# Opening pair of experts in the order gate, gate, up, up, down, with two up units in places used once

## The chip, the cores and the metric

One program runs on one core of a Trainium2 chip. The core has a matrix engine (TensorE, PE in the profile), a vector engine (VectorE, DVE), a scalar engine (ScalarE, ACT), GpSimd (POOL) and SyncE (SP), whose queue issues nearly all transfers from HBM to SBUF. Sixteen DMA engines carry these transfers. The metric is the device time of the program in microseconds (us), the median of several runs.

## The reference, cut to what matters

Two layers over 256 tokens of width 1024, in float32: a recurrent block with a dense feed-forward block, then attention with an expert block. Only the expert block is touched here: 8 experts, each token goes to its best two, and each expert is a SwiGLU of width 3584.

```python
def swiglu(h, w_gate, w_up, w_down):
    return (jax.nn.silu(h @ w_gate) * (h @ w_up)) @ w_down
...
    logits = (t @ router).astype(jnp.float32)
    top_v, top_i = lax.top_k(logits, TOP_K)
    w = jax.nn.softmax(top_v, axis=-1)
...
    for e in range(N_EXPERTS):
        out = out + combine[:, e:e + 1].astype(t.dtype) * swiglu(t, w_gate[e], w_up[e], w_down[e])
```

The weights of the 8 experts are 24 matrices of 1024 x 3584 float32, 14.7 MB each, 352 MB in all.

## The kernel before

**Units.** Each expert matrix is cut in eight units of 1792 KB, one DMA each, so an expert block has 192 loads. A gate or up unit is 128 rows of the matrix, and all eight are summed in PSUM. A down unit is three and a half "rows" of a [128 x 28 x 1024] view; the half row is finished with the next unit, so an even down unit is given back a little late.

**Pairs.** Experts are sorted by the number of their tokens and handled in four pairs: one large (96 token slots, 3 groups of 32) and one small (64 slots, 2 groups). Below, GL, UL and DL are the gate, up and down units of the large expert (0 to 7 each), GS and US those of the small one. Down units of the small expert are computed in the next pair (DE, "EARLIER" in the code). A pair in the middle takes its 48 units in the order GL, DE 0 to 3, UL, DE 4 to 7, GS, DL 0 to 3, US, DL 4 to 7. The opening pair has no DE, hence 40 units: GL, UL, GS, DL 0 to 3, US, DL 4 to 7. Its large expert is always expert 1 (`FIRST`), so it can be loaded before routing is known; the small one can't.

**Places.** A unit lies in one of 8 places of a ring (`PERMANENT`), 7 of them in the tensor `ring` and one `ring_last`. A load into a place waits until TensorE has used the unit that lay there (semaphore `used`, which counts finished units), so a new load is issued at each finished unit, in order. The first eleven units of the opening are loaded while attention still runs, each as soon as its memory is free: eight in the ring, three in places that are used once, `ring_a`, `ring_b` and `ring_c` (`BESIDE_A` to `BESIDE_C`). When a unit in such a place is finished, no load follows. `OPENED` says where the eleven lie: GL 0 and 1, GL 2 in `ring_b`, GL 3, GL 4 in `ring_a`, GL 5 to 7, UL 0 and 1, UL 2 in `ring_c`.

**Order.** Each engine runs its own list, written by hand. SP issues loads in the order in which TensorE takes the units (`pair_loads` for all but the eleven). On TensorE, `summed` computes a gate or up unit, `lowered` a down unit; `pair` is the order of a pair. PSUM banks 0 to 5 hold the three sums of the large expert, banks 0 to 3 the two of the small one, so the next matrix waits until ScalarE (`silus`) or VectorE (`products`) has read each bank pair (`acc_free`). `selection_transposes` prepares the scatter to tokens; `gather` fetches the tokens of the next pair in the midst of DL 4 and 5.

Of the kernel before, what the change touches and what calls it, by code (L numbers as in the profile page):

```python
# [24 lines left out]
KT = D // P  # L25
# [4 lines left out]
UK = 4  # L30
# [3 lines left out]
E = 8  # L34
# [62 lines left out]
def downs(job, steps):  # L97

    return [("D", job, n) for n in steps]


def pair_units(opening):

    def sums(kind, job):
        return [(kind, job, n) for n in range(KT)]
    early, late = (range(EARLY), range(EARLY, PARTS))
    return (sums("G", LARGE) + ([] if opening else downs(EARLIER, early)) + sums("U", LARGE)
            + ([] if opening else downs(EARLIER, late)) + sums("G", SMALL) + downs(LARGE, early)
            + sums("U", SMALL) + downs(LARGE, range(EARLY, PARTS)))


OPENING_UNITS, UNITS = pair_units(True), pair_units(False)
LAST_UNITS = downs(EARLIER, range(PARTS))
PAIR_UNITS = len(UNITS)
assert PAIR_UNITS % RING == 0 and len(OPENED) == RING + 3


class Group:
# [16 lines left out]
    def col(self, later=0):  # L135
        return at(2 * (self.ahead + later), 2, self.i)

    def later(self, i):
        return self.before + i - len(OPENED)

    def slot(self, i):
        n = self.later(i)
        return OPENED[n] if n < 0 else PERMANENT[n % RING]

    def landed(self, i):
        n = self.later(i)
        return 16 if n < 0 else at(16 * (n // RING + 2), 16 * PAIR_UNITS // RING, self.i)

    def free(self, i):
        n = self.later(i)  # L150
# [18 lines left out]
def hybrid_trunk(nc, x, norm_mix, norm_ffn, lru_w_in, lru_conv_w, lru_conv_b, lru_w_a, lru_b_a, lru_w_x, lru_b_x,  # L169
                 lru_log_lambda, lru_w_out, fox_w_in, fox_b_f, fox_q_gain, fox_k_gain, fox_w_out, ffn_w_gate,  # L170
                 ffn_w_up, ffn_w_down, moe_router, moe_w_gate, moe_w_up, moe_w_down, out):
    with ExitStack() as ctx:
# [138 lines left out]
        def of_group(a):  # L311
# [37 lines left out]
        arrived = [sem(f"arrived{i}") for i in range(len(OPENED))]  # L349
# [47 lines left out]
        def _(sp):  # L397
# [24 lines left out]
            def pair_loads(group):  # L422
                experts = {LARGE: slice(FIRST, FIRST + 1)} if group is OPENING else {}
                for i, (kind, job, n) in enumerate(group.table):
                    if group is OPENING and i < len(OPENED):
                        continue
                    if job not in experts:
                        if group is OPENING:
                            sp.wait_ge(listed, 1)
                        col = group.col(-1) + 1 if job == EARLIER else group.col() + job  # L430
                        experts[job] = bass.ds(sp.value_load(ids[0:1, bass.ds(col, 1)], min_val=0, max_val=E - 1), 1)
                    sp.wait_ge(used, group.free(i))
                    load(group, i, experts[job])
# [6 lines left out]
                    else:  # L440
                        sp.wait_ge(used, n + 1)

            def open_unit(i):
                load(OPENING, i, slice(FIRST, FIRST + 1))

            dense_done(2, 3, 4, 5)
            open_unit(0)
            open_unit(1)
            sp.wait_ge(scored, 8)
            open_unit(2)  # L450
            dense_done(0, 1, 2)
            open_unit(3)
            sp.wait_ge(o_T, 4)
            open_unit(4)
            dense_done(11, 12)
            open_unit(5)
            dense_done(6, 7)
            open_unit(6)
            dense_done(7, 8, 9)
            open_unit(7)  # L460
            dense_done(9, 10, 11)
            open_unit(8)
# [68 lines left out]
        def _(act):  # L531
# [252 lines left out]
            def silus(group, job):  # L784
                for a in range(GROUPS[job]):
                    if a < GROUPS[job] - 1:
                        act.wait_ge(m_part, group.nth((1, 5)[job] + a, 6))
# [14 lines left out]

            def pair(group, following):
                silus(group, LARGE)
                if group is not OPENING:
                    y_copy(SMALL, group.through("D", EARLIER, PARTS - 1))
                selection_copy(group, LARGE)
                silus(group, SMALL)
# [21 lines left out]
        def _(pe):  # L830
# [406 lines left out]

            def acc_free(group, kind, job, a):

                if kind == "U":  # L1240
                    pe.wait_ge(m_silu, group.nth((1, 4)[job] + a, ALL))
                elif job == SMALL:
                    pe.wait_ge(m_act, group.nth(1 + a, ALL))
                elif group is not OPENING and a < GROUPS[SMALL]:
                    pe.wait_ge(m_act, group.nth(a - 1, ALL))

            def summed(group, kind, job, n):
# [72 lines left out]
            def pair(group, following):  # L1320
                for n in range(KT):
                    if group is OPENING:
                        if n % UK == 0:
                            pe.wait_ge(m_x, 1 + n // UK)
                    elif n == 0:
                        pe.wait_ge(m_x, group.nth(2, 2))
                    summed(group, "G", LARGE, n)
                if group is not OPENING:
                    lowered_earlier(group, range(EARLY))
                for n in range(KT):  # L1330
                    summed(group, "U", LARGE, n)
                if group is not OPENING:
                    lowered_earlier(group, range(EARLY, PARTS))
                for n in range(KT):
                    summed(group, "G", SMALL, n)
                    if n == 1 and group is not OPENING:
                        scatter(group)
                    if n == 4:
                        pe.wait_ge(m_Sw, group.nth(1))
                        if group is OPENING:  # L1340
                            pe.wait_ge(m_act, group.nth(3, ALL))
                        else:
                            pe.wait_ge(m_acc, group.nth(0))
                        selection_transposes(group, LARGE)
                pe.wait_ge(m_aT, group.nth(GROUPS[LARGE], ALL))
                for n in range(EARLY):
# [4 lines left out]
                for n in range(KT):  # L1351
                    summed(group, "U", SMALL, n)
                for n in range(EARLY, PARTS):
                    lowered(group, LARGE, n)
                    if following is not None and n < EARLY + 2:
                        if n == EARLY:
                            pe.wait_ge(m_ST, group.nth(2, 2))
                            pe.wait_ge(m_S, following.nth(1))
                        else:
                            pe.wait_ge(m_x, following.nth(1, 2))  # L1360
                        gather(following, n - EARLY)

            pe.wait_ge(m_S, 1)
            pe.wait_ge(hn_hi_done, 2)
            gather_part(0, 4, hn_hi, True, False)
# [4 lines left out]
            pair(OPENING, SECOND)  # L1370
# [26 lines left out]
        def _(dve):  # L1397
# [498 lines left out]
            def products(group, job):  # L1896
                for a in range(GROUPS[job]):
                    if a < GROUPS[job] - 1:
                        dve.wait_ge(m_part, group.nth((3, 6)[job] + a, 6))
# [9 lines left out]
            def pair(group, following):  # L1909
# [3 lines left out]
                products(group, LARGE)  # L1913
                if group is not OPENING:
                    accumulate(group)
                if following is not None:
                    one_hot(group, following)
                products(group, SMALL)

            pair(OPENING, SECOND)  # L1920
            pair(SECOND, Group(0, 2))
# [44 lines left out]
```

## Time and profile before

| | us |
|---|---|
| median of 3 runs | 1338.05 (1337.34 to 1338.09) |
| the profiled execution's own time | 1338.2 |
| its span | 1336.4 |
| PE busy | 1271.3 (95%) |
| DVE busy | 363.3 (27%) |
| ACT busy | 284.5 (21%) |
| POOL busy | 30.9 (2%) |
| HBM read over the span | 325 GB/s in the mean |

The profile cuts the span into 40 slices of 33.4 us; the rows on DMA and on GB/s say for each how busy the 16 DMA engines were, in tenths, and what they moved. A matrix multiplication in float32 stands in the trace as two records, so a unit of GL or UL (24 instructions) is 48 records and one of GS or US (16 instructions) is 32. The queue of SP shows when a load was issued; another view says how long it took from there to its landing.

### The profile page before, as it was taken

Reading aid. Unit: us, or ns where it says so; the run is one execution under the profiler, and the core shown is the slowest. Engines: PE = TensorE matmul, PEld = TensorE weight load, DVE = VectorE, ACT = ScalarE, POOL = GpSimd, SP = SyncE. Lnnn points to the kernel's source line nnn. Section 1 sums busy time; section 2 is a strip of 40 time slices with the busy share of each in tenths; the row PEclk is TensorE's granted clock in tenths of the full one; section 3 lists DMA queues with packets and bytes.
Section 4 is the critical chain, followed back from the end, with each engine's and each line's share of the span. In section 5 each row is a group of like instructions: output and inputs, shape, how many; then the busy total and the mean of one; then the engine's idle time right before and its main releaser. Section 6 shows DMA issues by size and latency. Waiting matters only on the chain.

```text
span 1336.4 us, 27795 instructions
## 1 busy us (share of the span) xinstructions
PE 1271.3 (95%) x12897; PEld 766.0 (57%) x12897; DVE 363.3 (27%) x470; ACT 284.5 (21%) x357; POOL 30.9 (2%) x34
## 2 busy tenths in 40 slices
PE   7999999999999999999999999899998799989897
PEld 7978888888888884335534434344344254344344
DVE  6976444445654363020100200100110100020010
ACT  5855444443545530000000000000000000000000
POOL 2000000000230000000000000000000000000000
PEclk9999999999999999999999999999999999999999
DMA  9556555554441298899999999999999999999994
GB/s 338 171 167 227 185 184 184 188 188 157 157 127 64 87 424 339 319 401 425 426 425 425 425 425 425 427 424 426 426 424 426 426 425 426 425 425 425 425 425 198
DMA packets 70323, 435.53 MB, mean 326 GB/s; under 512 B 4656, under 2 KB 6816, under 8 KB 45632
## 3 DMA queue, kind: packets, MB, share of 16 engines
q1 hardware_dynamic: 69744, 433.10, 81.0%
q8 instruction: 101, 1.65, 0.5%
q0 software_dynamic: 368, 0.63, 0.2%
q14 instruction: 14, 0.11, 0.0%
q10 hardware_dynamic: 96, 0.03, 0.0%
HBM read 432.69 MB, written 1.05 MB: 325 GB/s over the span
## 4 chain that ended last, share of the span: by engine, by line
PE 73%; DMA 23%; ACT 2%; DVE 1%; issue 1%; SPq 0%; POOL 0%; DVEq 0%; ACTq 0%
PE ps L1258 25%; DMA ring<-in_moe_w_down_dram 16%; PE ps L1275 13%; PE ps L839 9%; PE ps L841 9%; PE ps L840 9%; DMA ring<-in_moe_w_gate_dram 6%; PE ps L1229 1%; PE ps L1069 1%; PE ps L1096 1%; PE ps L855 1%; PE ps L881 1%; PE ps L871 1%; PE ps L868 1%; PE ps L870 1%
## 5 line engine op out<-in xcount | busy, mean ns | idle before, releaser
L1258 PE MATMUL ps<-ring,xg 128*32 128x512 f32 (+1 forms) x4384 | 423.1, 540 | 26.6 <-DMA ring<-in_moe_w_up_dram 16.1
L1258 PEld LDWEIGHTS ps<-ring,xg 128*32 128x32 f32 x4384 | 140.1, 110 | 299.6 <-issue 251.3
L1423 DVE TENSOR_TENSOR wlo<-raw,whi 128x2048 fp32r<-128x2048 f32 x73 | 166.5, 2287 | 74.2 <-PE ps L841 72.2
L541 ACT ACTIVATE whi<-raw 128x2048 fp32r<-128x2048 f32 x73 | 139.3, 1916 | 85.3 <-PE ps L841 83.8
L839 PE MATMUL ps<-whi,hT_hi 128*128 128x512 f32 x384 | 153.4, 399 | 2.4 <-DVE wlo L1423 1.4
L841 PE MATMUL ps<-whi,hT_lo 128*128 128x512 f32 x384 | 149.9, 390 | 0.0
L840 PE MATMUL ps<-wlo,hT_hi 128*128 128x512 f32 x384 | 149.7, 390 | 0.0
L1275 PE MATMUL ps<-ring,aTL 128*32 128x256 f32 x2352 | 133.9, 380 | 7.3 <-DMA ring<-in_moe_w_down_dram 7.1
L1903 DVE TENSOR_TENSOR gtL<-gtL,ps 128x896 f32<-128x896 f32 x12 | 13.1, 1089 | 368.3 <-PE ps L1258 368.3
L1275 PEld LDWEIGHTS ps<-ring,aTL 128*32 128x32 f32 x2352 | 77.6, 110 | 59.8 <-DMA ring<-in_moe_w_down_dram 7.8
L1275 PE MATMUL ps<-ring,aTS 128*32 128x256 f32 x1568 | 90.2, 380 | 10.7 <-DMA ring<-in_moe_w_down_dram 9.7
L839 PEld LDWEIGHTS ps<-whi,hT_hi 128*128 128x128 f32 x384 | 72.2, 188 | 18.3 <-issue 3.1
L841 PEld LDWEIGHTS ps<-whi,hT_lo 128*128 128x128 f32 x384 | 72.1, 188 | 15.3
L840 PEld LDWEIGHTS ps<-wlo,hT_hi 128*128 128x128 f32 x384 | 72.3, 188 | 13.7
L1275 PEld LDWEIGHTS ps<-ring,aTS 128*32 128x32 f32 x1568 | 51.9, 110 | 46.9 <-DMA ring<-in_moe_w_down_dram 14.1
L1258 PE MATMUL ps<-ring_last,xg 128*32 128x512 f32 (+1 forms) x592 | 58.5, 540 | 3.2 <-DMA ring_last<-in_moe_w_up_dram 3.2
L1903 DVE TENSOR_TENSOR gtS<-gtS,ps 128x896 f32<-128x896 f32 x8 | 8.7, 1087 | 176.3 <-PE ps L1258 176.3
L795 ACT ACTIVATE yS<-ps 128x512 f32<-128x512 f32 x4 | 2.4, 597 | 217.1 <-PE ps L1275 217.1
L839 PE MATMUL ps<-whi,fT_hi 128*128 128x512 f32 x112 | 44.9, 401 | 0.0
L840 PE MATMUL ps<-wlo,fT_hi 128*128 128x512 f32 x112 | 44.3, 395 | 0.0
L841 PE MATMUL ps<-whi,fT_lo 128*128 128x512 f32 x112 | 44.3, 395 | 0.0
L1258 PEld LDWEIGHTS ps<-ring_last,xg 128*32 128x32 f32 x592 | 18.8, 110 | 40.2 <-issue 34.9
(292 smaller groups left out, 1016.9 us busy)
## 6 DMA issues: line engine op xcount, KB each, us to landing
ring<-in_moe_w_down_dram SPq DMA_DIRECT2D x56, 1792.0 KB, 29.1
ring<-in_moe_w_gate_dram SPq DMA_DIRECT2D x55, 1792.0 KB, 27.5
ring<-in_moe_w_up_dram SPq DMA_DIRECT2D x55, 1792.0 KB, 24.8
raw<-in_fox_w_in_dram SPq DMA_DIRECT2D x16, 1024.0 KB, 5.4
raw<-in_ffn_w_gate_dram SPq DMA_DIRECT2D x14, 1024.0 KB, 5.1
raw<-in_ffn_w_up_dram SPq DMA_DIRECT2D x14, 1024.0 KB, 5.1
raw<-in_ffn_w_down_dram SPq DMA_DIRECT2D x14, 1024.0 KB, 5.1
ring_last<-in_moe_w_up_dram SPq DMA_DIRECT2D x8, 1792.0 KB, 27.3
```

The lines of the kernel that those rows point to most:

```text
L541: nc.scalar.activation(whi[:, m % HR], raw[:, DENSE[m]], ACT.Copy).then_inc(hi_done, 1)
L839: mm(dst(t), hi, whi[:, m % HR, k * CW:(k + 1) * CW], start=first and k == 0, stop=False)
L840: mm(dst(t), hi, wlo[:, m % LR, k * CW:(k + 1) * CW], start=False, stop=False)
L841: ins = mm(dst(t), lo, whi[:, m % HR, k * CW:(k + 1) * CW], start=False, stop=last and k == UK - 1)
L855: ins = mm(dst, raw[:, 0, k * CW + c * P:k * CW + (c + 1) * P], h_f[:, k], start=k == 0 and c % 2 == 0, stop=False, skip_group_check=True)
L868: mm(dst, wh, hT_hi[:, kk], start=half == 0 and k == 0 and c % 2 == 0, stop=False, skip_group_check=True)
L870: mm(dst, wh, hT_lo[:, kk], start=False, stop=False, skip_group_check=True)
L871: ins = mm(dst, wl, hT_hi[:, kk], start=False, stop=half == 1 and k == UK - 1, skip_group_check=True)
L1258: ins = mm(ps[strip(c), 2 * a + b, 0:width], x, w[:, c * STRIP + first:c * STRIP + first + width], start=n == 0, stop=n == KT - 1, skip_gr ...
L1275: ins = mm(ps[strip(c), 6 + a // 2, quarter(a % 2)], aTs[small][:, r, held(a)], places[group.slot(held_in)][:, first:first + QUARTER], sta ...
L1423: nc.vector.tensor_tensor(wlo[:, m % LR], raw[:, DENSE[m]], whi[:, m % HR].bitcast(F32), ALU.subtract).then_inc(lo_done, 1)
L1903: nc.vector.tensor_tensor(gts[job][:, a], gts[job][:, a], of_group(a), ALU.mult).then_inc(m_act, 1)
```

## The change

The opening pair takes its 40 units in the order GL, GS, UL, US, DL 0 to 7. The pairs after it keep theirs. Of the eleven units loaded ahead, eight are in the ring (GL 0, 1, 2, 4, 5, 6, 7 and GS 0) and three in the places used once: GL 3 in `ring_a`, UL 0 in `ring_b`, UL 1 in `ring_c`. GS 0 belongs to an expert that routing chooses, so SP waits for `listed` in place of `routed` and reads the expert's number before it issues that load. The waits on banks, the order of ScalarE (silu of the small expert right after that of the large one) and of VectorE (products of the small one ahead of `one_hot`) follow. The two transposes of the selection move with the order: those of the large expert behind US 4, those of the small one stay behind DL 1.

```diff
-OPENED = (1, 2, BESIDE_B, 0, BESIDE_A, 6, 3, 4, 5, 7, BESIDE_C)
...
+OPENING_UNITS = sums("G", LARGE) + sums("G", SMALL) + sums("U", LARGE) + sums("U", SMALL) + downs(LARGE, range(PARTS))
...
+ONCE = {OPENING_UNITS.index(("G", LARGE, 3)): BESIDE_A, OPENING_UNITS.index(("U", LARGE, 0)): BESIDE_B,
+        OPENING_UNITS.index(("U", LARGE, 1)): BESIDE_C}
+RINGED = [i for i in range(len(OPENING_UNITS)) if i not in ONCE]
+AHEAD = {*RINGED[0:RING], *ONCE}
...
     def free(self, i):
-        n = self.later(i)
-        return N_MOE + OPENED.index(PERMANENT[n]) + 1 if n < RING else self.units(i - RING + 1)
+
+        return self.units(i - RING + 1 if self.ahead else RINGED[self.turn(i) - RING] + 1)
...
-            sp.wait_ge(routed, 1)
-            open_unit(9)
+            open_unit("G", 7)
+            sp.wait_ge(listed, 1)
+            small = sp.value_load(ids[0:1, OPENING.col() + SMALL:OPENING.col() + SMALL + 1], min_val=0, max_val=E - 1)
+            open_unit("G", 0, SMALL, bass.ds(small, 1))
             sp.wait_ge(hn_hi_done, 2)
             sp.wait_ge(hn_lo_done, 2)
-            open_unit(10)
+            open_unit("U", 1)
...
+                if group is OPENING:
+                    if job == SMALL:
+                        pe.wait_ge(m_silu if kind == "G" else m_act, 1 + a)
+                    elif kind == "U":
+                        pe.wait_ge(m_silu, 4 + a if a < GROUPS[SMALL] else 1 + a)
...
+            def opening_pair():
+
+                for n in range(KT):
+                    if n % UK == 0:
+                        pe.wait_ge(m_x, 1 + n // UK)
+                    summed(OPENING, "G", LARGE, n)
+                for n in range(KT):
+                    summed(OPENING, "G", SMALL, n)
+                for n in range(KT):
+                    summed(OPENING, "U", LARGE, n)
+                for n in range(KT):
+                    summed(OPENING, "U", SMALL, n)
+                    if n == 4:
+                        pe.wait_ge(m_Sw, 1)
+                        pe.wait_ge(m_act, 3)
+                        selection_transposes(OPENING, LARGE)
+                lowered_large(OPENING, range(EARLY))
+                lowered_with_gather(OPENING, SECOND)
```

The order of SP's queue where the opening is loaded, before. `ring`, `ring_last` and `ring_a` to `ring_c` are the places.

```order
L420 DMA ring_b<-in_moe_w_gate_dram 128x3584 [waits scored]
L420 DMA ring<-in_moe_w_gate_dram 128x3584 [waits lo_done]
L420 DMA ring_a<-in_moe_w_gate_dram 128x3584 [waits o_T]
L420 DMA ring<-in_moe_w_gate_dram 128x3584 [waits used] x3
L420 DMA ring<-in_moe_w_up_dram 128x3584 [waits used]
L420 DMA ring_last<-in_moe_w_up_dram 128x3584 [waits routed]
L420 DMA ring_c<-in_moe_w_up_dram 128x3584 [waits hn_lo_done,hn_hi_done]
L420 DMA ring<-in_moe_w_up_dram 128x3584 [waits used] x5
L431 TENSOR_LOAD ids [waits listed]
```

The same stretch of SP's queue in the changed kernel.

```order
L425 DMA ring_b<-in_moe_w_up_dram 128x3584 [waits scored]
L425 DMA ring<-in_moe_w_gate_dram 128x3584 [waits lo_done]
L425 DMA ring_a<-in_moe_w_gate_dram 128x3584 [waits o_T]
L425 DMA ring<-in_moe_w_gate_dram 128x3584 [waits used] x4
L469 TENSOR_LOAD ids [waits listed]
L469 ISA x2
L425 ISA
L425 DMA ring_last<-in_moe_w_gate_dram 128x3584
L425 DMA ring_c<-in_moe_w_up_dram 128x3584 [waits hn_lo_done,hn_hi_done]
L436 TENSOR_LOAD ids [waits listed]
```

An up unit now takes the third turn and a gate unit of the small expert the tenth, behind the read of its number; the loads that wait for a finished unit come behind both, seven gates of the small expert first and the other six up units of the large one next, where five up units and eight gates stood.

TensorE where the first matrix ends, before: the last gate unit of the large expert, then UL 0, then UL 1 in `ring_last`.

```order
L1258 MATMUL ps<-ring,xg 32x512 [waits m_silu,arrived5]
L1258 MATMUL ps<-ring,xg 32x512 x3
L1258 MATMUL ps<-ring,xg 32x384 x4
L1258 MATMUL ps<-ring,xg 32x512 [waits m_silu]
...
L1258 MATMUL ps<-ring_last,xg 32x512 [waits arrived7]
```

The same place in the changed kernel: GS 0, with two groups, in `ring_last`, then GS 1.

```order
L1272 MATMUL ps<-ring_last,xg 32x512 [waits m_silu,arrived7]
L1272 MATMUL ps<-ring_last,xg 32x512 x3
L1272 MATMUL ps<-ring_last,xg 32x384 x4
L1272 MATMUL ps<-ring_last,xg 32x512 [waits m_silu]
...
L1272 MATMUL ps<-ring,xg 32x512 [waits arrived1]
```

The units of two groups, 16 instructions each, follow the first matrix directly, and each of them gives a ring place back.

## Rows read from the trace of the kernel before

**Rows 1.** The page, the 40 slices: DMA busy in tenths, and GB/s.
```profile
DMA  9556555554441298899999999999999999999994
GB/s 338 171 167 227 185 184 184 188 188 157 157 127 64 87 424 339 319 401 425 426 425 425 425 425 425 427 424 426 426 424 426 426 425 426 425 425 425 425 425 198
```
**Rows 2.** The chain that ended last, in order of time: start, us, what.
```profile
625.12 24.05 PE ps L1258 x256
...
671.79 36.08 PE ps L1258 x384
...
747.22 27.29 DMA ring<-in_moe_w_gate_dram
...
1296.10 29.33 DMA ring<-in_moe_w_down_dram
```
**Rows 3.** Stretches of 50 us: engines' busy time, PE clock, DMA share, GB/s.
```profile
590.00:640.00 50.00, 50.00 (x740) 23.44 (x736) 1.88 (x9) 3.24 (x4) 0.00 (x0) 1.00 1.01 426
...
1240.00:1290.00 50.00, 41.91 (x564) 17.15 (x556) 5.77 (x4) 0.00 (x0) 0.00 (x0) 1.00 1.01 424
```
**Rows 4.** The same view in stretches of 10 us, at the start of the expert block.
```profile
470.00:480.00 10.00, 10.00 (x49) 8.20 (x48) 7.14 (x12) 1.09 (x2) 0.63 (x1) 1.00 0.99 417
...
520.00:530.00 10.00, 10.00 (x112) 3.50 (x108) 0.00 (x0) 0.00 (x0) 0.00 (x0) 1.00 0.72 255
530.00:540.00 10.00, 10.00 (x116) 3.42 (x110) 0.00 (x0) 0.00 (x0) 0.00 (x0) 1.00 0.61 221
540.00:550.00 10.00, 10.00 (x112) 3.50 (x108) 0.00 (x0) 2.75 (x3) 0.00 (x0) 1.00 0.94 350
...
560.00:570.00 10.00, 10.00 (x112) 3.47 (x108) 0.00 (x0) 0.00 (x0) 0.00 (x0) 1.00 0.74 264
570.00:580.00 10.00, 10.00 (x112) 3.46 (x108) 1.77 (x2) 0.00 (x0) 0.00 (x0) 1.00 1.00 384
```
**Rows 5.** SP's queue: start of a run of issues, its length, place and matrix, count.
```profile
506.30 0.33 SPq L420 DMA_DIRECT2D ring_c<-in_moe_w_up_dram  x1
...
513.16 27.39 SPq L420 DMA_DIRECT2D ring<-in_moe_w_up_dram  x5
...
544.88 0.36 SPq L420 DMA_DIRECT2D ring<-in_moe_w_gate_dram  x1
...
580.95 0.33 SPq L420 DMA_DIRECT2D ring<-in_moe_w_gate_dram  x1
...
628.19 9.35 SPq L420 DMA_DIRECT2D ring<-in_moe_w_down_dram  x4
640.36 3.34 SPq L420 DMA_DIRECT2D ring<-in_moe_w_gate_dram  x2
...
671.99 0.33 SPq L420 DMA_DIRECT2D ring<-in_moe_w_gate_dram  x1
...
707.93 0.33 SPq L420 DMA_DIRECT2D ring<-in_moe_w_up_dram  x1
```
**Rows 6.** Us from issue to landing: of 496.55, 526.69, 544.88, 580.95, 671.99 and 707.93.
```profile
ring_last<-in_moe_w_up_dram SPq DMA_DIRECT2D x1, 1792.0 KB, 16.0
...
ring<-in_moe_w_up_dram SPq DMA_DIRECT2D x1, 1792.0 KB, 7.1
...
ring<-in_moe_w_gate_dram SPq DMA_DIRECT2D x1, 1792.0 KB, 9.2
...
ring<-in_moe_w_gate_dram SPq DMA_DIRECT2D x1, 1792.0 KB, 9.8
...
ring<-in_moe_w_gate_dram SPq DMA_DIRECT2D x1, 1792.0 KB, 23.7
...
ring<-in_moe_w_up_dram SPq DMA_DIRECT2D x1, 1792.0 KB, 22.2
```
**Rows 7.** VectorE, timeline: the write of the experts' numbers, which releases `listed`.
```profile
501.89 0.17 DVE L1804 CAST ids<-ranked 128x8 int32<-128x8 f32 x1
```
**Rows 8.** ScalarE, timeline: the first silu of the large expert.
```profile
541.73 0.92 ACT L790 ACTIVATE gtL<-ps 128x896 f32<-128x896 f32 x1 [31.24 <-PE ps L1258]
```

More of the change, by code:

```diff
@@ L99, in downs, with sums @@
     return [("D", job, n) for n in steps]
[L102 to L112, printed above, removed]
+def sums(kind, job):
+    return [(kind, job, n) for n in range(KT)]
+OPENING_UNITS = sums("G", LARGE) + sums("G", SMALL) + sums("U", LARGE) + sums("U", SMALL) + downs(LARGE, range(PARTS))
+UNITS = (sums("G", LARGE) + downs(EARLIER, range(EARLY)) + sums("U", LARGE) + downs(EARLIER, range(EARLY, PARTS))
+         + sums("G", SMALL) + downs(LARGE, range(EARLY)) + sums("U", SMALL) + downs(LARGE, range(EARLY, PARTS)))
 LAST_UNITS = downs(EARLIER, range(PARTS))
 PAIR_UNITS = len(UNITS)
-assert PAIR_UNITS % RING == 0 and len(OPENED) == RING + 3
+ONCE = {OPENING_UNITS.index(("G", LARGE, 3)): BESIDE_A, OPENING_UNITS.index(("U", LARGE, 0)): BESIDE_B,
+        OPENING_UNITS.index(("U", LARGE, 1)): BESIDE_C}
+RINGED = [i for i in range(len(OPENING_UNITS)) if i not in ONCE]
+AHEAD = {*RINGED[0:RING], *ONCE}
+assert PAIR_UNITS % RING == 0 and KT == RING
 class Group:
@@ L136, in col, with turn @@
         return at(2 * (self.ahead + later), 2, self.i)
-    def later(self, i):
-        return self.before + i - len(OPENED)
+    def turn(self, i):
+        if self.ahead:
+            return self.before + i - len(ONCE)
+        return RINGED.index(i)
     def slot(self, i):
-        n = self.later(i)
-        return OPENED[n] if n < 0 else PERMANENT[n % RING]
+        if not self.ahead and i in ONCE:
+            return ONCE[i]
+        return PERMANENT[self.turn(i) % RING]
     def landed(self, i):
-        n = self.later(i)
-        return 16 if n < 0 else at(16 * (n // RING + 2), 16 * PAIR_UNITS // RING, self.i)
+        if not self.ahead and i in ONCE:
+            return 16
+        return at(16 * (self.turn(i) // RING + 1), 16 * PAIR_UNITS // RING, self.i)
     def free(self, i):
-        n = self.later(i)
-        return N_MOE + OPENED.index(PERMANENT[n]) + 1 if n < RING else self.units(i - RING + 1)
+        return self.units(i - RING + 1 if self.ahead else RINGED[self.turn(i) - RING] + 1)
 def last_dense(place):
@@ L348, in hybrid_trunk @@
             sem(s) for s in ("m_act", "m_aT", "m_acc", "m_S", "m_Sw", "m_col", "m_tab", "m_fin"))
-        arrived = [sem(f"arrived{i}") for i in range(len(OPENED))]
+        arrived = [sem(f"arrived{i}") for i in range(RING + len(ONCE))]
         out_done, sumsq_v, par_in2, ff_T = sem("out_done"), sem("sumsq_v"), sem("par_in2"), sem("ff_T")
@@ L424, in pair_loads @@
                 for i, (kind, job, n) in enumerate(group.table):
-                    if group is OPENING and i < len(OPENED):
+                    if group is OPENING and i in AHEAD:
                         continue
@@ L441, in dense_done, with open_unit @@
                         sp.wait_ge(used, n + 1)
-            def open_unit(i):
-                load(OPENING, i, slice(FIRST, FIRST + 1))
+            def open_unit(kind, n, job=LARGE, expert=slice(FIRST, FIRST + 1)):
+                load(OPENING, OPENING.place[kind, job, n], expert)
             dense_done(2, 3, 4, 5)
-            open_unit(0)
-            open_unit(1)
+            open_unit("G", 0)
+            open_unit("G", 1)
             sp.wait_ge(scored, 8)
-            open_unit(2)
+            open_unit("U", 0)
             dense_done(0, 1, 2)
-            open_unit(3)
+            open_unit("G", 2)
             sp.wait_ge(o_T, 4)
-            open_unit(4)
+            open_unit("G", 3)
             dense_done(11, 12)
-            open_unit(5)
+            open_unit("G", 4)
             dense_done(6, 7)
-            open_unit(6)
+            open_unit("G", 5)
             dense_done(7, 8, 9)
-            open_unit(7)
+            open_unit("G", 6)
             dense_done(9, 10, 11)
-            open_unit(8)
-            sp.wait_ge(routed, 1)
-            open_unit(9)
+            open_unit("G", 7)
+            sp.wait_ge(listed, 1)
+            small = sp.value_load(ids[0:1, OPENING.col() + SMALL:OPENING.col() + SMALL + 1], min_val=0, max_val=E - 1)
+            open_unit("G", 0, SMALL, bass.ds(small, 1))
             sp.wait_ge(hn_hi_done, 2)
             sp.wait_ge(hn_lo_done, 2)
-            open_unit(10)
+            open_unit("U", 1)
             pair_loads(OPENING)
@@ L786, in silus @@
                     if a < GROUPS[job] - 1:
-                        act.wait_ge(m_part, group.nth((1, 5)[job] + a, 6))
+                        act.wait_ge(m_part, group.nth((1, 3 if group is OPENING else 5)[job] + a, 6))
                     else:
@@ L804, in pair @@
                 silus(group, LARGE)
-                if group is not OPENING:
+                if group is OPENING:
+                    silus(group, SMALL)
+                else:
                     y_copy(SMALL, group.through("D", EARLIER, PARTS - 1))
                 selection_copy(group, LARGE)
-                silus(group, SMALL)
+                if group is not OPENING:
+                    silus(group, SMALL)
                 selection_copy(group, SMALL)
@@ L1238, in acc_free @@
             def acc_free(group, kind, job, a):
-                if kind == "U":
+                if group is OPENING:
+                    if job == SMALL:
+                        pe.wait_ge(m_silu if kind == "G" else m_act, 1 + a)
+                    elif kind == "U":
+                        pe.wait_ge(m_silu, 4 + a if a < GROUPS[SMALL] else 1 + a)
+                elif kind == "U":
                     pe.wait_ge(m_silu, group.nth((1, 4)[job] + a, ALL))
@@ L1243, in acc_free @@
                     pe.wait_ge(m_act, group.nth(1 + a, ALL))
-                elif group is not OPENING and a < GROUPS[SMALL]:
+                elif a < GROUPS[SMALL]:
                     pe.wait_ge(m_act, group.nth(a - 1, ALL))
@@ L1318, in selection_transposes, with lowered_large @@
                 ins.then_inc(m_TS, 1)
[L1320 to L1346, printed above, removed]
+            def lowered_large(group, steps):
+                for n in steps:
+                    if n == 0:
+                        pe.wait_ge(m_aT, group.nth(GROUPS[LARGE], ALL))
                     lowered(group, LARGE, n)
@@ L1350, in pair, with lowered_with_gather @@
                         selection_transposes(group, SMALL)
-                for n in range(KT):
-                    summed(group, "U", SMALL, n)
+            def lowered_with_gather(group, following):
                 for n in range(EARLY, PARTS):
@@ L1361, in pair @@
                         gather(following, n - EARLY)
+            def opening_pair():
[15 more added lines that the diff above has]
+                lowered_with_gather(OPENING, SECOND)
+            def pair(group, following):
+                for n in range(KT):
+                    if n == 0:
+                        pe.wait_ge(m_x, group.nth(2, 2))
+                    summed(group, "G", LARGE, n)
+                lowered_earlier(group, range(EARLY))
+                for n in range(KT):
+                    summed(group, "U", LARGE, n)
+                lowered_earlier(group, range(EARLY, PARTS))
+                for n in range(KT):
+                    summed(group, "G", SMALL, n)
+                    if n == 1:
+                        scatter(group)
+                    if n == 4:
+                        pe.wait_ge(m_Sw, group.nth(1))
+                        pe.wait_ge(m_acc, group.nth(0))
+                        selection_transposes(group, LARGE)
+                lowered_large(group, range(EARLY))
+                for n in range(KT):
+                    summed(group, "U", SMALL, n)
+                lowered_with_gather(group, following)
             pe.wait_ge(m_S, 1)
@@ L1369, in _ @@
             gather_part(1, 6, hn_lo, False, True).then_inc(m_gat, 1)
-            pair(OPENING, SECOND)
+            opening_pair()
             pair(SECOND, Group(0, 2))
@@ L1898, in products @@
                     if a < GROUPS[job] - 1:
-                        dve.wait_ge(m_part, group.nth((3, 6)[job] + a, 6))
+                        dve.wait_ge(m_part, group.nth((4 if group is OPENING else 3, 6)[job] + a, 6))
                     else:
@@ L1915, in pair @@
                     accumulate(group)
+                if group is OPENING:
+                    products(group, SMALL)
                 if following is not None:
                     one_hot(group, following)
-                products(group, SMALL)
+                if group is not OPENING:
+                    products(group, SMALL)
             pair(OPENING, SECOND)
```

## The prediction

> **What bounds the kernel now.** I read the slices first. From slice 19 on (about 600 us) the transfers move 424 to 427 GB/s in every slice but the last [rows 1], at a DMA share of 1.01 in the first stretch of 50 us and in the last full one, and in the twelve between them [rows 3]. The chain of waits seems to speak against that: around 625 and 671 us it runs on TensorE alone, and only from 747.22 us on in loads [rows 2]. But the load issued at 747.22 took 27.29 us, and one that found an empty queue took 7.1 [rows 6]. It stood some 20 us behind other loads; had it been issued sooner, it would have landed no sooner. So from about 590 us the end is set by how many bytes are still to be moved. The last load lands at 1296.10 + 29.33 = 1325.43 [rows 2], 11 us ahead of the span's end.
>
> What can be won is therefore DMA time ahead of that point, and the 10 us stretches show it: 255, 221, 350, 264 and 384 GB/s, where later 425 are moved [rows 4]. Five stretches of ten, without the one at 550: (170 + 204 + 75 + 161 + 41) / 425 x 10 = 15 us of transfer that did not take place. TensorE is busy for all of each of them, so it is not short of data. SP is short of free places. A unit of GL or UL takes 36.08 / 8 = 4.51 us on TensorE, one of GS or US 24.05 / 8 = 3.01 [rows 2], and a load that comes into a full queue costs the stream this: between the load issued at 580.95, landed 590.75 (GS 7), and the one issued at 671.99, landed 695.69, lie 24 loads [rows 5, 6], so 104.9 / 24 = **4.37 us a load**. The same rate holds to the end: 168 loads from 590.75 to 1325.43 are 4.37 each. Large units give places back at 4.51, more slowly than the transfers could fill them, and each unit in a place used once (GL 2, GL 4, UL 2) gives none back, a hole of 4.5 us. Small units give one back every 3.01 us and would let a queue build up, but they only begin at 580.95.
>
> **The change, part by part.**
>
> *The first refills.* The eleven loads ahead are issued at the same moments as before and end at the same one: the eleventh waits for the same two semaphores. Then come 13 loads, each released by a finished unit. Before, all 13 were released by large units, 16 units apart with the three holes: the first at 513.16, the last at 580.95 (that is 15 x 4.51 later), which lands at 590.75 [rows 5, 6]. Now GL 0, 1, 2 and 4 to 7 release GS 1 to 7. GL 7 is finished at the same 544.7 us as before (the issue at 544.88, [rows 5]), and that load took 9.2 us with another 4.5 us ahead of it [rows 6], so **GS 7 lands at 554.0**. The six next, UL 2 to 7, are released by GS 0 to 5 at 547.8, 550.8 and so on to 562.8, every 3.01 us, faster than 4.37. The queue is full from there, and the 13th load lands at 554.0 + 6 x 4.37 = **580.2**. That is 590.75 - 580.2 = 10.6 us sooner.
>
> *Does the queue stay full?* The bounds on a load in a thin queue are 7.1 us (empty queue) and 9.2 to 9.8 (one load ahead of it) [rows 6]; for this step I take 9.2. UL 0 and UL 1 are in places used once, so between GS 7 (finished 568.9) and UL 2 (finished 582.4) no place comes free for 13.5 us. The two loads released last before that gap, US 0 and US 1, are due at 584.6 and 588.9; US 2, issued at 582.4, is due at 593.3, 10.9 us after its issue. From there to US 7 the releases come every 4.51 us against 4.37 due: US 7 is issued at 605.0 and due at 615.2, 10.2 us. That is above 9.2 by 1.0 us, the tightest place. Then the eight US units release every 3.01 us, and the queue grows again. In the second pair TensorE is where it was, since the opening holds the same 40 units and the same transposes. The load issued at 671.99 has 23.7 - 10.6 = 13.1 us left to its landing, that at 707.93 has 22.2 - 10.6 = 11.6 [rows 6]; this is the least of that pair. So up to 22.2 - 9.2 = 13.0 us of gain fit through the ring, and 10.6 do.
>
> The first hole moves too: GL 3 gives no place back, so no load is issued between about 522.2 and 531.2. It is one hole where three were, and the later two fall where a queue stands.
>
> In a sentence of its own: the Trainium skill ("DMA: Bandwidth & Descriptors", Anatomy of one DMA) fits one DMA on the GpSimd path as 2.0 us plus bytes / 436e3, which gives 6.2 us for 1792 KB, as an estimate. By that figure GS 7 would land at about 551 and the gain would be some 13.6 us, cut to about 13 by the ring; the trace, with 7.1 and 9.2 to 9.8 us on SP's queue, does not bear the 6.2 out.
>
> *Does TensorE have its data?* GS 7 is wanted at 565.9 and lands at 554.0; UL 2 is wanted at 577.9 and lands at 558.4; US 7 is wanted at about 627 (2 us of it transposes) and lands at 615.2; DL 0 lands 4.4 us behind and is wanted at 630. No wait.
>
> *The banks.* GS 0 wants the banks of the large gate, as UL 0 did before: no difference. UL 0 now wants the first bank pair from GS 7: its second group takes 1.5 us on TensorE, and the silu between takes 0.92 us [rows 8], so 0.6 us to spare. US 0 wants a product of UL 7 with two groups (3.0 us) to cover it. All at nothing. If such a cover were gone, 1 us of TensorE would come off the 1.0 us of the tightest place and cost nothing or a few tenths.
>
> *SP's read.* GS 0's load now waits for `listed`, at 501.89 + 0.17 = 502.06 [rows 7], in place of the 496.55 of its turn before, and for the read of a register. A like read stands between the issues that end at 637.54 and start at 640.36 [rows 5], so it takes under 2.8 us: the load goes out by 504.9. The stream then still works on loads that are due until about 508 (the one issued at 496.55 landed at 512.55, one load later, [rows 6]), and a load is due 7.1 us after issue at the earliest: 512.0, against 512.55. It is hidden, by half a microsecond at the least; without that cover it costs up to 2 us. Behind it in SP's queue stands only the load into `ring_c`, which goes out at 506.30 anyway [rows 5].
>
> *ScalarE, VectorE, POOL.* Both silus and both products come sooner, and one_hot a little later; the gather that wants it stands behind DL 4, three down units (13 us) after the transposes that start it. Off the path. POOL has no part.
>
> **The sum.** 1338.2 (span 1336.4 and 1.8 around it) - 10.6 = 1327.6 for a profiled execution. The median of the runs is 0.15 lower: **1327.4 us**.
>
> **The rivals.**
>
> *The queue stays empty less long than I count (more gain).* If loads at 4.5 us apart took 7.1 us, GS 7 would land at 551.8 and the gain be 12.7: 1325.3. For it: a load behind a hole took 7.1. Against: GS 7 is the fourth load in a row at 4.5 us. Chance 10%.
>
> *A thin queue is a slow queue (slower).* In the stretch 570 to 580 the DMA share is 1.00 and yet only 384 GB/s are moved [rows 4]: 4.37 x 425 / 384 = 4.84 us a load, 0.47 more. Now loads stand 10 to 15 us in the queue from 582 to about 745 us, where they stood 10 to 28; that is (745 - 582) / 4.37 = 37 loads, 17.5 us in all, and the kernel would end at 1327.4 + 17.5 = 1345. From 23 such loads on it is slower than before. Against it: at 470 to 480, soon after the first of the eleven loads, 417 GB/s were moved [rows 4]. Chance 4%. A weak form of it (a fifth of that price, 3.5 us, or a hole at the tightest place) has 9%: 1330.9.
>
> *The late read of the expert's number opens a hole ahead of 513 us*, where the queue is about to run dry: 2 to 3 us, 1330. Chance 5%.
>
> *No change.* The chain of waits is right, TensorE sets the end up to 747 us, and an order of the same units moves nothing: 1338. Against it stand 20 us of queue in the load at 747.22. The same result would come if the loads ahead did not all land where I put them. Chance 3%.
>
> **How the numbers follow.** The forecast, 8.5 to 12 us of gain, has 69%; more gain 10%; a weak loss in the thin queue or at SP 14%; no change 3%; slower 4%. The range, 1325.0 to 1331.0, leaves out the last two and some of the edges. What a measurement of this kernel can tell from no change is 0.2%, 2.7 us. Faster by over that: 0.93; within: 0.03; slower: 0.04.
>
> **What the profile after would show.** The DMA rows at 530 to 580 us: one thin stretch near 525 to 545, then 410 GB/s or more from 550 on. The issues after 544.7 come 3.01 us apart. The load of UL 7 (issued 562.8) lands at 580, some 17 us after issue. The load issued at about 672 lands near 685, after 13 us in place of 23.7; that at 708 after 11 to 12. TensorE still reaches the second pair at 672. The last load lands at 1315. I am wrong if the thin queue at 582 to 610 shows under 405 GB/s, if the load of GS 0 lands after 513.5, or if the first silu of the small expert holds TensorE up.

## The result and the profile after

The changed kernel takes **1327.99 us** (median of 4 runs, 1327.27 to 1329.03) against 1337.69 for the kernel before (1336.94 to 1338.09) in the same session: ratio **0.9929, 95% interval 0.9912 to 0.9946**. Forecast were 1327.4 and 1325.0 to 1331.0. The profiled execution has a span of 1325.8 us, 10.6 below the 1336.4 of before.

The DMA rows of its page, 40 slices of 33 us, answer to [rows 1]:

```profile
DMA  9546555555442199999999999999999999999994
GB/s 332 181 164 225 184 189 190 191 189 160 159 128 65 43 421 393 383 426 426 424 426 425 426 424 425 426 426 425 425 425 424 426 425 425 426 425 426 425 425 188
```

The slices 339, 319, 401 of before are now 393, 383, 426. In stretches of 10 us (engines' busy time, PE clock, DMA share, GB/s), against [rows 4]:

```profile
520.00:530.00 10.00, 10.00 (x116) 3.42 (x109) 0.00 (x0) 0.00 (x0) 0.00 (x0) 1.00 0.80 330
530.00:540.00 10.00, 10.00 (x112) 3.48 (x108) 0.00 (x0) 0.00 (x0) 0.00 (x0) 1.00 0.89 318
540.00:550.00 10.00, 10.00 (x112) 3.44 (x108) 0.00 (x0) 2.75 (x3) 0.00 (x0) 1.00 0.96 376
550.00:560.00 10.00, 10.00 (x112) 3.45 (x108) 0.00 (x0) 0.00 (x0) 0.00 (x0) 1.00 1.01 429
...
570.00:580.00 10.00, 10.00 (x108) 3.38 (x104) 0.00 (x0) 0.00 (x0) 0.00 (x0) 1.00 1.01 426
...
590.00:600.00 10.00, 10.00 (x112) 3.50 (x108) 0.00 (x0) 0.00 (x0) 0.00 (x0) 1.00 1.00 425
```

The transfers are full from 550 us on, in place of about 590. Only the stretch from 520 to 550 is still thin. SP's queue (start of the issue, its length, place and matrix) shows the releases that do it: GL 0 finished, the load behind the hole at GL 3, GL 7 finished, UL 2 and UL 7 issued, US 7, and the two of the second pair that [rows 5] show at 671.99 and 707.93:

```profile
511.90 0.35 SPq L425 DMA_DIRECT2D ring<-in_moe_w_gate_dram  x1
...
529.92 0.33 SPq L425 DMA_DIRECT2D ring<-in_moe_w_gate_dram  x1
...
543.45 0.33 SPq L425 DMA_DIRECT2D ring<-in_moe_w_gate_dram  x1
546.32 0.34 SPq L425 DMA_DIRECT2D ring_last<-in_moe_w_up_dram  x1
...
561.35 0.33 SPq L425 DMA_DIRECT2D ring<-in_moe_w_up_dram  x1
...
603.45 0.33 SPq L425 DMA_DIRECT2D ring<-in_moe_w_up_dram  x1
...
670.57 0.33 SPq L425 DMA_DIRECT2D ring<-in_moe_w_gate_dram  x1
...
706.51 0.33 SPq L425 DMA_DIRECT2D ring<-in_moe_w_up_dram  x1
```

and how long from issue to landing, for six of them in order (543.45, 546.32, 561.35, 603.45, 670.57, 706.51), against [rows 6]:

```profile
ring<-in_moe_w_gate_dram SPq DMA_DIRECT2D x1, 1792.0 KB, 9.3
...
ring_last<-in_moe_w_up_dram SPq DMA_DIRECT2D x1, 1792.0 KB, 10.8
...
ring<-in_moe_w_up_dram SPq DMA_DIRECT2D x1, 1792.0 KB, 17.2
...
ring<-in_moe_w_up_dram SPq DMA_DIRECT2D x1, 1792.0 KB, 10.6
...
ring<-in_moe_w_gate_dram SPq DMA_DIRECT2D x1, 1792.0 KB, 13.6
...
ring<-in_moe_w_up_dram SPq DMA_DIRECT2D x1, 1792.0 KB, 12.3
```

The chain of waits (start, us, what) has also changed:

```profile
507.04 111.38 PE ps L1272 x1184
...
818.94 27.12 DMA ring<-in_moe_w_down_dram
...
1284.69 29.32 DMA ring<-in_moe_w_down_dram
```

It stays on TensorE until 818 us, 71 us longer than in [rows 2]. That alone is no sign of a TensorE that became the bound: loads land 10 us sooner while TensorE is where it was, so it catches up with them later. How much TensorE may be late there is what r7 measures.

**A clock for the comparison.** Two profiled executions don't reach the expert block at the same moment. GL 0 is finished at 513.16 in the profile before and at 511.90 in that after, and over all profiles of this study between 511.6 and 513.7, whichever kernel it is. So I count from there: from the load that GL 0 releases to the last landing. Before: 1325.43 - 513.16 = **812.3 us**. After: 1314.01 - 511.90 = **802.1 us**. Repeats of the changed kernel gave 802.0 and 802.2, and two executions of one other version (r5 and r12) 800.8 and 800.3, so this figure is good to some 0.5 us, where the medians move by a microsecond. The 10.6 us between the two spans are 10.2 of this stretch and 1.3 of an earlier start, less 0.8 that the program now takes longer behind its last load.

### The profile page after: what moved, and what is told of

Its sections match the earlier page's. It is cut to its first block, busy times and chain, and to the rows that moved or that the text cites. A ratio compares the mean times of both kernels' runs of the same rounds, so it can differ in the third digit from the quotient of the medians.

```text
span 1325.8 us, 27799 instructions
## 1 busy us (share of the span) xinstructions
PE 1267.3 (96%) x12897; PEld 764.0 (58%) x12897; DVE 363.1 (27%) x470; ACT 284.5 (21%) x357; POOL 30.9 (2%) x34
## 4 chain that ended last, share of the span: by engine, by line
PE 78%; DMA 18%; ACT 2%; DVE 1%; issue 0%; SPq 0%; POOL 0%; DVEq 0%
PE ps L1272 27%; PE ps L1289 14%; DMA ring<-in_moe_w_down_dram 14%; PE ps L848 9%; PE ps L850 9%; PE ps L849 9%; DMA ring<-in_moe_w_gate_dram 4%; PE ps L1238 1%; PE ps L1078 1%; PE ps L1105 1%; PE ps L864 1%; PE ps L890 1%; PE ps L877 1%; PE ps L880 1%; PE ps L879 1%
## 5 line engine op out<-in xcount | busy, mean ns | idle before, releaser
L1272 PE MATMUL ps<-ring,xg 128*32 128x512 f32 (+1 forms) x4384 | 421.5, 540 | 21.1 <-DMA ring<-in_moe_w_up_dram 13.7
L1937 DVE TENSOR_TENSOR gtL<-gtL,ps 128x896 f32<-128x896 f32 x12 | 13.1, 1088 | 404.2 <-PE ps L1272 404.2
L849 PEld LDWEIGHTS ps<-wlo,hT_hi 128*128 128x128 f32 x384 | 72.2, 188 | 13.7
```

The costliest lines, as they stand in the source:

```text
L849: mm(dst(t), hi, wlo[:, m % LR, k * CW:(k + 1) * CW], start=False, stop=False)
L1272: ins = mm(ps[strip(c), 2 * a + b, 0:width], x, w[:, c * STRIP + first:c * STRIP + first + width], start=n == 0, stop=n == KT - 1, skip_gr ...
L1937: nc.vector.tensor_tensor(gts[job][:, a], gts[job][:, a], of_group(a), ALU.mult).then_inc(m_act, 1)
```

## The experiments

All figures "to the last landing" count as just said. Each run was timed beside the kernel before.

**The changed kernel again (r1).** No edit.

> The changed kernel again, as the mark for the three beside it. Theory (what counts is how early loads are issued while the transfers are not full): 1328.0 us, 9.7 below before, the 13th load after the first finished unit lands 66.6 us after that unit. No rival differs here.

1327.44 us, ratio 0.9921 (0.9905 to 0.9938), 802.0 us to the last landing.

**The places alone (r2).** The kernel before, with this order of places and the loads ahead issued to fit:

```diff
-OPENED = (1, 2, BESIDE_B, 0, BESIDE_A, 6, 3, 4, 5, 7, BESIDE_C)
+OPENED = (1, 2, 0, BESIDE_A, 6, 3, 4, 5, BESIDE_B, BESIDE_C, 7)
```

> The order of before (GL, UL, GS, DL, US, DL) with the places of after: GL 3, UL 0 and UL 1 in the places used once, the ring for the rest. Theory: the 13th load is still released by UL 7, some 68 us after the first finished unit, and lands 9 to 10 us later, so nothing is gained: 1337.7 us, within 0.8. Rival (half of the gain comes from which units stand in the places used once, and the holes they leave): 1333 us or less.

1336.68 us, ratio 0.9994 (0.9984 to 1.0003), 812.2 us to the last landing against 812.3. GS 7 lands 77.6 us after GL 0's release, as before. The places alone bring nothing: the 13th load is released by UL 7 in both.

**The order alone (r3).** The changed kernel with these places, and the loads ahead issued to fit:

```diff
-ONCE = {OPENING_UNITS.index(("G", LARGE, 3)): BESIDE_A, OPENING_UNITS.index(("U", LARGE, 0)): BESIDE_B,
-        OPENING_UNITS.index(("U", LARGE, 1)): BESIDE_C}
+ONCE = {OPENING_UNITS.index(("G", LARGE, 2)): BESIDE_B, OPENING_UNITS.index(("G", LARGE, 4)): BESIDE_A,
+        OPENING_UNITS.index(("U", LARGE, 0)): BESIDE_C}
```

and GS 0 and GS 1 both loaded ahead.

> The order of after with the places of before: GL 2 and GL 4 in places used once and, as the eleventh load ahead, UL 0 in the third. Theory: now only 6 loads are released by GL 7 in place of 7, and the full stretch starts one load poorer, so 4.4 us of the gain go: 1332.4 us. Rival (the order brings it all, the places nothing, as r2 would suggest if read alone): 1328 us.

1331.49 us, ratio 0.9954 (0.9937 to 0.9970), 806.6 us to the last landing: 4.5 more than the changed kernel (802.1), forecast 4.4. So the order alone brings 5.7 of the 10.2 us, and the places, which alone bring nothing, bring 4.5 on top of it. A hole in the releases costs a load (4.4 us) where the transfers wait for releases, and nothing where they have a queue. Only the new order makes such a place behind GL 7.

**Ten loads ahead (r4).** `ONCE` without `("U", LARGE, 1)`, and UL 0 in `BESIDE_C`.

> The changed kernel with ten loads ahead in place of eleven: UL 0 goes into the place of UL 1, and UL 1 is an ordinary load; one of the three places stays unused. Theory: one load more comes behind the full stretch's start, at 4.37 us: 1332.4 us. Rival (the queue has room and swallows it, since one hole in the releases goes too): 1328 us.

1331.91 us, ratio 0.9958 (0.9941 to 0.9974), 806.3 us to the last landing: 4.3 more than r1. One place used once is worth one load.

**The hole elsewhere (r5, and r12 again).** GL 6 in place of GL 3 stands in a place used once, and GL 3 to 5 are loaded ahead one turn later each:

```diff
-ONCE = {OPENING_UNITS.index(("G", LARGE, 3)): BESIDE_A, OPENING_UNITS.index(("U", LARGE, 0)): BESIDE_B,
+ONCE = {OPENING_UNITS.index(("G", LARGE, 6)): BESIDE_A, OPENING_UNITS.index(("U", LARGE, 0)): BESIDE_B,
```

> The changed kernel with GL 6 in the first place used once in place of GL 3, so the one hole in the releases of GL lies between GL 5 and GL 7, 9 us before the last. As many loads (7) are released by GL 7. Theory: the load released by GL 7 finds a nearly empty queue and lands 7.0 us after issue in place of 9.3; the queue of UL allows 1.4 us of this (10.6 us left there against 9.2 wanted): 1326.6 us. Rival (only the number of loads issued by GL 7 counts): 1328.0 us.

> r5 again, beside r10 and r11 on the same chip: 1326.4 us. Theory: 1.0 above r11. Rival: the same as r11.

1326.30 us, ratio 0.9925 (0.9907 to 0.9942), and 1325.99, ratio 0.9923 (0.9909 to 0.9936); 800.8 and 800.3 us to the last landing, 1.2 to 1.8 less than the changed kernel. The load that GL 7 releases, in r5:

```profile
543.39 0.33 SPq L425 DMA_DIRECT2D ring<-in_moe_w_gate_dram  x1
...
ring<-in_moe_w_gate_dram SPq DMA_DIRECT2D x1, 1792.0 KB, 7.1
```

It lands after 7.1 us in place of 9.3. The size of the gain is in the bytes, in stretches of 10 us of r5:

```profile
520.00:530.00 10.00, 10.00 (x112) 3.47 (x108) 0.00 (x0) 0.00 (x0) 0.00 (x0) 1.00 0.99 379
530.00:540.00 10.00, 10.00 (x112) 3.42 (x108) 0.00 (x0) 0.00 (x0) 0.00 (x0) 1.00 1.01 413
540.00:550.00 10.00, 10.00 (x112) 3.50 (x108) 0.00 (x0) 2.75 (x3) 0.00 (x0) 1.00 0.77 290
```

379 + 413 + 290 against 330 + 318 + 376: 58 more, 58 / 425 x 10 = 1.4 us of transfer.

**GS 0 late (r6).** `sp.wait_ge(counted, 1)` in place of `listed`.

> The changed kernel, but SP issues the load of GS 0 only when the counts of the experts are there (about 511.7 us) in place of 502, and UL 1 behind it, so the transfers run dry for some 8 us ahead of the first finished unit. Theory: these two go first at 512, the seven refills behind them fill the thin stretch, GS 7 lands at 554.2 in place of 552.8: 1329.4 us. Rival (a hole ahead of the refills costs its length): 1335 us or more.

1329.49 us, ratio 0.9949 (0.9931 to 0.9967). GS 0 goes out at 512.47, 10.8 us late, and the load that GL 7 releases lands 12.0 us after its issue in place of 9.3:

```profile
512.47 0.35 SPq L425 DMA_DIRECT2D ring_last<-in_moe_w_gate_dram  x1
...
ring<-in_moe_w_gate_dram SPq DMA_DIRECT2D x1, 1792.0 KB, 12.0
```

803.9 us to the last landing (GL 0's own release is hidden here; it is put 4.5 us ahead of that of GL 1, at 516.17), so 1.9 us more than r1 (1.7 more than r8) for a read 10.8 us late. The thin stretch behind took in the rest: at 520 to 550 this run moved 426 to 429 GB/s. My forecast was 1.4, at 1329.4 us by the median.

**More work for TensorE (r7, r9).** In the gather of the second pair, in DL 4 of the opening, of the changed kernel (r7) and of the kernel before (r9):

```diff
+                if group is SECOND and half == 0:
+                    for _ in range(5):
+                        gather_part(half, 4, hn_hi, True, False)
```

> The changed kernel with the first eight matrix multiplications of the gather of the second pair done six times in place of once, in DL 4 of the opening: 5.3 us more for TensorE at about 651 us, same result. Theory: loads stand 12.3 us in the queue at 706 us and want 9.2, so 3.1 us are hidden and 2.2 show: 1330.2 us. Rival (TensorE sets the end up to 815 us, as the chain of waits has it): 1333.3 us. Second rival (full queue, nothing shows): 1328.0 us.

> The kernel before with the same 5.3 us more for TensorE in DL 4 of the opening as r7. Theory: loads stand 22 us in the queue there, so all of it is hidden and nothing shows: 1337.7 us. Rival (TensorE sets the end, as the chain of waits of before has it from 549 to 747 us): 1343.0 us.

The timeline of TensorE in r7 shows 48 records where 8 stood:

```profile
651.80 6.02 PE L1238 MATMUL ps<-S,hn_hi 128*128 128x256 f32 x48
657.66 1.12 PE L1238 MATMUL ps<-S,hn_lo 128*128 128x256 f32 x8
```

They are 4.8 us more, not the 5.3 I had written. The chain of waits has the gather in it, in the kernel before and in r9:

```profile
653.06 2.10 PE ps L1229 x16
...
651.77 6.90 PE ps L1229 x56
```

**r9: 1337.17 us, ratio 1.0000 (0.9991 to 1.0010)**, 812.5 us to the last landing against 812.3. Nothing shows, though the longer piece lies on the chain of waits. **r7: 1328.81 us, ratio 0.9940 (0.9922 to 0.9958)**, 803.1 us to the last landing, 0.9 to 1.1 more than the three profiles of the changed kernel: about 1 of the 4.8 shows, where I had forecast 2.2. The medians alone (1328.33 in r8, the changed kernel beside it) could not tell this from nothing. Right behind the late gather the transfers of r7 are thin, in stretches of 5 us:

```profile
670.00:675.00 5.00, 5.00 (x98) 2.99 (x92) 0.00 (x0) 0.00 (x0) 0.00 (x0) 1.00 0.87 319
675.00:680.00 5.00, 5.00 (x60) 1.82 (x56) 0.00 (x0) 0.81 (x1) 0.00 (x0) 1.00 0.94 362
...
685.00:690.00 5.00, 5.00 (x60) 1.75 (x56) 0.00 (x0) 0.00 (x0) 0.00 (x0) 1.00 1.02 408
```

The load that stood 12.3 us in the queue at 706 us, in r7:

```profile
711.55 0.33 SPq L425 DMA_DIRECT2D ring<-in_moe_w_up_dram  x1
...
ring<-in_moe_w_up_dram SPq DMA_DIRECT2D x1, 1792.0 KB, 8.5
```

So loads 4.5 us apart went down to 8.5 us from issue to landing, where I had taken 9.2 as the least; with 12.3 - 8.5 = 3.8 us of the 4.8 hidden, about 1 us is left to show, as it did. By this number the change spent 10 of the 14 us that TensorE could be late there.

**The same work one pair later (r8).** The extra work was to come where `group.ahead == 2 and group.i is None`, and no group of this kernel meets that: the timeline shows the gather at 850.06 with its 8 records, and no more. r8 is the changed kernel a third time, and neither its theory nor its rival was tried.

> The changed kernel with the same 5.3 us more for TensorE one pair later, at about 850 us, where loads stand over 24 us in the queue. Theory: nothing shows, 1328.0 us. Rival (TensorE sets the end, the chain of waits runs over it there too): 1333.3 us.

1328.33 us, ratio 0.9938 (0.9920 to 0.9956), 802.2 us to the last landing. What extra TensorE time does at 850 us was not tried.

**Later units in the places used once (r10), and with the late hole (r11).**

```diff
-        ... OPENING_UNITS.index(("U", LARGE, 0)): BESIDE_B,
-        OPENING_UNITS.index(("U", LARGE, 1)): BESIDE_C}
+        ... OPENING_UNITS.index(("U", LARGE, 7)): BESIDE_B,
+        OPENING_UNITS.index(("U", SMALL, 3)): BESIDE_C}
```

> The changed kernel with later units in two of the places used once: UL 7 in place of UL 0, US 3 in place of UL 1 (GL 3 stays). The ring then gets a place back at every UL unit but the last, and the loads released in UL go out 4.5 to 9 us sooner. The queue at 580 to 605 us is deeper (15 us in place of 11), but the stretch ahead of 554 us, which sets the end, is the same. Theory: 1327.5 us, 0 to 0.5 below the changed kernel. Rival (every sooner release is a gain): 1323 us.

> r10 with GL 6 in place of GL 3 as well. In r5 the load behind the late hole landed 2.3 us sooner, but the queue at 599 to 603 us stood at 9.1 us and let only 1.2 of them through. Theory: with the deeper queue of r10 the rest comes through, 1325.4 us, some 1.0 below r5 and 2.2 below the changed kernel. Rival (the end has another limit at about r5's): 1326.3 us.

r10: 1328.42 us, ratio 0.9937 (0.9924 to 0.9951), 802.0 us to the last landing. The queue is deeper, as meant: US 7 was issued 82.5 us behind GL 0's release (512.44 in this profile) and stood 19.4 us, where the changed kernel issued it 91.5 behind, at 603.45, and it stood 10.6:

```profile
594.97 0.33 SPq L425 DMA_DIRECT2D ring<-in_moe_w_up_dram  x1
...
ring<-in_moe_w_up_dram SPq DMA_DIRECT2D x1, 1792.0 KB, 19.4
```

and nothing is gained by it. r11: 1326.16 us, ratio 0.9920 (0.9906 to 0.9933), 800.8 us to the last landing, the same as r5 and r12. My theory for r11 fell and its rival held. In r5 I had put the missing 1.1 us (the load behind the hole 2.2 sooner, the end only 1.2) to the thin queue at 603 us. But in r5 the 13th load lands 65.5 us behind GL 0's release, and in r11 and r12 too, against 66.6 and 66.7 in the changed kernel and r1 (67.7 in r8). So the 1.2 us that the end shows were won by 578 us and none was lost behind it. A load into an empty queue lands sooner than its share of the stream; the bytes of the stretch say what is won.

The late hole (r5, r12, r11) is the best run here. By the last landing it beats the changed kernel by 1.2 to 1.8 us; by the ratios it can't be told from it.

## Why the prediction was right, step by step

- **The bound.** Transfers, not TensorE, set the end of the kernel before from the first full stretch on. r9 shows it for one place and 4.8 us: so much more on TensorE where the chain of waits stands on it, and no change. For later places it is argued, from loads that stand over 20 us in the queue. In the changed kernel the margin is smaller: about 1 us of the same 4.8 shows (r7).
- **GS 7 lands 40.8 us behind GL 0's release** (554.0 - 513.16). Measured 543.45 + 9.3 - 511.90 = 40.9.
- **The 13th load lands at 67.0** (580.2 - 513.16). Measured 561.35 + 17.2 - 511.90 = 66.7, against 77.6 before: 10.9 us sooner, forecast 10.6.
- **It stays won.** US 7 was to be 10.2 us in the queue, measured 10.6; the load near 672 was to have 13.1, measured 13.6; that near 708 was to have 11.6, measured 12.3. At the end 10.2 of the 10.9 are left. The rate behind the 13th load is (1314.01 - 578.55) / 168 = 4.38 us a load against 4.37. The 0.7 between is less than what repeats differ by at the 13th load: it lands at 66.7 in r1 and at 67.7 in r8, and both end within 0.2 us of the changed kernel's 802.1. So nothing can be said of where it went.
- **Mis-sized: the bound on a load in a thin queue.** I took 9.2 us; r7 shows 8.5. So the ring would let 13.7 us of gain through, not 13.0. It did not matter for 10. The bound for an empty queue was read from one load, 7.1 us, and is no single number either: in the kernel before, a load issued at 535.71, when every load before it had landed (at 533.8), took 8.3.

```profile
535.71 0.33 SPq L420 DMA_DIRECT2D ring<-in_moe_w_up_dram  x1
...
ring<-in_moe_w_up_dram SPq DMA_DIRECT2D x1, 1792.0 KB, 8.3
```

- **TensorE has its data, and the banks cost nothing.** TensorE runs through from 507.04 to 818 us with no piece of a load in the chain. The two silus of the small expert stand at 565.87 and 567.37, 0.92 us each, inside the two groups' work.
- **SP's read.** GS 0 was to go out by 504.9 at the latest and went out at 501.66 (the numbers are there at 500.65 in this profile), so the read takes about 1 us. Of the rival "a late read opens a hole, 2 to 3 us" r6 shows the price: 1.9 us for 10.8 us of lateness. So such a hole does cost, but 2 to 3 us for a read that is a few microseconds late was too much; a delay of that size was not run.
- **The slow thin queue.** 425 to 429 GB/s from 550 us on, with loads that stand 10.6 to 13 us in it. The 384 GB/s at a share of 1.00 of [rows 4] do not come back there. That rival is gone for a queue of 10 us and more. Below that something like it is left: in r7, where loads stood 8.9 to 9.5 us, 408 GB/s were moved at a share of 1.02. What makes a full share move less was not tried.
- **The fit of the page.** The Trainium skill ("DMA: Bandwidth & Descriptors", Anatomy of one DMA) gives 6.2 us as an estimate for 1792 KB on its path, that of GpSimd. Loads that SP issued into an empty queue took 6.9 to 8.6 here, so it is under them all.
- **Outside the sum.** The stretch behind the last load grew by 0.8 us (below), and the start was 1.3 us earlier by chance. They cancel in part; 10.2 - 0.8 = 9.4 is what the change is worth, and the medians say 9.7.

## What to carry to other kernels

Where the transfers are full to the end, look for the last moment at which they were not, and ask what would have let one more load go out before it; each such load is worth its own transfer time, 4.4 us here. Buffers that are used once belong where a queue of loads stands, and units that are quick to compute belong where there is none. And read a long wait for a load in the chain against the time of a load in a thin queue: 27 us against 8.5 says that this load could have been issued some 18 us later (an estimate; 4.8 us was tried). The least such margin over all the loads behind the place counts, and a change that brings the loads forward uses it up.

## What the runs showed of the hardware

**The last landing waits for the slowest of the 16 engines.** In stretches of 5 us, the end of the changed kernel's loads:

```profile
1295.00:1300.00 5.00, 5.00 (x100) 3.00 (x95) 0.00 (x0) 0.00 (x0) 0.00 (x0) 1.00 0.76 322
1300.00:1305.00 5.00, 3.27 (x64) 1.69 (x52) 0.00 (x0) 0.00 (x0) 0.00 (x0) 1.00 0.52 218
1305.00:1310.00 5.00, 4.30 (x76) 2.40 (x80) 0.00 (x0) 0.00 (x0) 0.00 (x0) 1.00 0.52 215
1310.00:1315.00 5.00, 3.10 (x60) 1.64 (x56) 0.00 (x0) 0.00 (x0) 0.00 (x0) 1.00 0.20 83
```

From 1300 us on half of the engines have nothing left: the trace has 8 packets under way at a time, where it had 16 up to 1296, and a packet of 14336 B takes 0.54 us as before. The last load lands at 1314.01. The bytes of these four stretches, (322 + 218 + 215 + 83) x 5 = 4190 us x GB/s, would take 4190 / 425 = 9.9 us with all engines at work, so by this estimate the loads would end at 1304.9, 9 us sooner. The skew builds up along the full stretch. For each load the trace holds 16 completions, and the load has landed with the last of them. From the first to the last of the 16 it is 2.1 us for the load that lands at 578.5, 6.7 us for the one at 789.0 and 17.1 us for the last load; eight of its 16 come 12.7 us or more ahead of the landing, the other eight within 2.9. The kernel before ends with 16.8. So 4.38 us a load is the pace of the slower eight; by the first completion of each load it is 4.29 over the same 168 loads. The skew is nearly as large as the gain of this change. What makes some engines slower was not tried.

**0.8 us behind the last load.** From the first issue of the output to the end of the span the profiles of before, r2 and r9 take 4.7 us, those of all runs with the new order 5.0 to 5.6. The output goes out in four transfers; the last takes 2.9 us to its landing in the changed kernel and 2.1 in the kernel before. One packet of instructions comes in both programs near the end, at 1337.4 us in the kernel before, 1.0 us behind the end of its span, and at 1323.8 us in the changed one, between the issue of the last output at 1322.5 and its landing. The queue in the stretches 1337 to 1338 us (before) and 1323 to 1324 us (changed):

```profile
q14 instruction: 1, 0.01, 2.2%
...
q14 instruction: 1, 0.01, 2.8%
```

It lies behind the span's end in r2 and r9 too, although r9 has 80 instructions more than the kernel before, and amid the output in every run with the new order. That the packet is the cause is only argued: both come with the changed program text, and no run took them apart.
